# Cached keys summed head by head inside the heads of a hybrid decoder layer, a pooling tile as filler of the last head, and the stage behind in a new order

## The chip, the cores and the metric

One core of one Trainium2 chip runs the whole layer as one program. The metric is the time of one execution on the device in microseconds (us), the median of several. Engines are called by their names or by the profile's: TensorE (PE, with PEld for its weight loads), VectorE (DVE), ScalarE (ACT), GpSimd (POOL) and SyncE (SP), which here only issues DMAs.

## The reference

One decoder layer serves 1024 prompt tokens and 8 sample tokens (one new token for each of 8 sequences that have 512 cached tokens). Per layer:

```python
h = rms_norm(x, g_mix); z = h @ w_in        # [pool 512 | q 1024 | k 1024 | v 1024 | two gates 2048]
q, k = rope(z[q]), rope(z[k])               # 8 heads, two maps (c) of 64 per head
s = einsum('bqhcd,bkhcd->bhcqk', q, k) * 64 ** -0.5   # samples: k, v = cached pages + own token
p = softmax(masked s); a = p[:, :, 0] - lam * p[:, :, 1]
o = rms_norm(einsum('bhqk,bkhe->bqhe', a, v), g_subln) * (1 - lam_init)
pool_out = pool_mixer(z[pool])              # windows 2/4/8/16, mean minus token, map per group, scale
merged = sigmoid(gate1) * (pool_out @ w_pool_proj) + sigmoid(gate2) * (o @ w_attn_proj)
x = x + merged @ w_o
x = x + square(relu(rms_norm(x) @ w_up)) @ w_down; y = rms_norm(x)
```

Outputs are y for both groups, the new keys and values, and the last 15 rows of the pooling input. All is float32. The cached keys and values lie in pages of 128 tokens x 8 heads x 128 numbers, 4 pages per sample, found through a page table.

## The kernel before

Every engine has its own program; all order between them is by semaphores (names `s_...`), written out by hand. Each large product is made of three passes of a float32 split into a high and a low part: high x high, high x low, low x high. ScalarE makes the high part of the weights (`w_hi`, L1038), VectorE the low part (`w_lo`, L1347, `next_low`). Tokens are the 1032 columns, in three chunks of 344 (`passes`, L666).

**Heads.** After the first norm comes a loop over 8 heads of 9 steps (`head`, on each engine). Step s of head h does scores of query tile s (L602, L606), maxima (L1233) and exponentials (L946), the weights of the two maps (`weights`, L1243 to L1248), their transposes (L625) with `aT_hi` and `aT_lo` (L953, L1255), the value product of tile s-2 (L635), and beside it the projection of q, k, v of token tile s for head h+1 (L580), which VectorE rotates (`rotate`, L1218 to L1222) and GpSimd completes (`rotated`, L1646 to L1650) into `kv_st`. A staging buffer `kv_st` per parity holds nine tiles; `store_kv` (L399 to L405) stores them when all nine are ready. At a head's start ScalarE and VectorE split the next projection weights (`split_qkv`, L916, L1182). The last head (h = 7) has no projection beside it; at its last step three thirds of the first pooling product are put in (`first_product`).

**The stage behind.** `PART_A` lists 16 tiles: u is the product of a group of pooling channels (8 blocks of k, 72 matmuls), grp its 128x128 map (9 matmuls), gate a tile of the first gate (72) and pool a tile of `w_pool_proj` (36). Four gates and four pools stand in that list and four more pairs in a loop behind it. Two sets of three PSUM banks alternate; a tile's set is released through `s_free`. `pooling` (L1368 to L1384) makes windows, `pooled_low` (L1389) the low part `pl_lo`, for which grp waits; `y_hi` (L1078) and `y_lo` (L1458) are the map's output. Gate tiles go through the one buffer `gate`.

The cached keys are worked on in this stage. For each sample b, `load_keys` brings four pages of 128 tokens x all heads (2 MB) into one of two slots of `kv_pages` and the sample's q, spread over partitions, into `q_bc`. GpSimd multiplies three pages (L1684), VectorE the fourth (L1406) and sums all of them (`sum_keys`, L1410) at the tiles that `REDUCE_AT` names. Behind the last sum come the samples' softmax (`sample_softmax`), `select_weights`, and then the cached values through the same two slots: VectorE weighs two pages (L1491), GpSimd two (L1690), VectorE adds them (L1498, L1500), TensorE sums over partitions (`cached_values`, L799). The own scores of the samples (`own_scores`, L1395 to L1400) come after the second u tile.

Then come the attention gates and projections, w_o, the MLP and the last norm, which the change leaves alone.

Of the kernel before, what the change touches and what calls it, by code (L numbers as in the profile page):

```python
# [12 lines left out]
P = 128  # L13
D = 1024
# [55 lines left out]
def decoder_layer(nc, ins, outs):  # L70
# [48 lines left out]
    kv_st, _ = put("kv_st", [P, 2, NTT + 1, 2, P], F32)  # L119
# [25 lines left out]
    end_attn = cursor[0]  # L145

# [18 lines left out]
    up, a = put("up", [P, PAD + TOK], F32, r3)  # L165
# [10 lines left out]
    smp_q, _ = put("smp_q", [P, D], F32, tmp)  # L176
    smp_k, _ = put("smp_k", [P, D], F32, r4 - 4 * D)
# [7 lines left out]
    q_bc = [put("q_bc0", [P, D], F32, slot2[1])[0], put("q_bc1", [P, D], F32, slot2[2])[0]]  # L185
# [5 lines left out]
    wg_raw, a = put("wg_raw", [P, NG, P], F32, max(a, end_attn))  # L191
    inv_n, a = put("inv_n", [P, 16], F32, a)
    us, a = put("us", [P, NG, DEC, 16], F32, a)
    ufix, ufix_end = put("ufix", [P, 32], F32, a)
    tail_st, a = put("tail_st", [P, D_POOL], F32, slot2[0])
    state, a = put("state", [P, D_POOL], F32, a)
    a = ufix_end
    sc_all, a = put("sc_all", [P, PAGES, P], F32, a)
    sm_w, a = put("sm_w", [P, PAST], F32, a)
    a_all, a = put("a_all", [P, PAGES, DEC * HEADS], F32, a)  # L200
    sel, a = put("sel", [P, DEC * HEADS], F32, a)
    eye8, a = put("eye8", [P, DEC], F32, a)
    own, a = put("own", [P, DEC, 16], F32, a)
    own_s, a = put("own_s", [P, 16], F32, a)
# [29 lines left out]
    with ExitStack() as ctx:  # L234
# [26 lines left out]
        s_kv = [sem(f"kv_stored{i}") for i in range(2)]  # L261
# [8 lines left out]
        s_prod2, s_vs, s_vp = sem("k_products_dve"), sem("v_steps"), sem("v_products")  # L270
# [51 lines left out]
        PG_K = 16 * (PAGES + 1) * DEC // 2  # L322
# [8 lines left out]
        SET = (3, 0)  # L331
# [19 lines left out]
        def gate_tile(i):  # L351
            return later(S_LOOP // 2 + i, 0)

        def pool_tile(i):
            return later(S_LOOP // 2 + i, 1)
# [25 lines left out]
        def _(sp):  # L381
# [14 lines left out]
            def store_kv(h, par):  # L396

                sp.wait_ge(s_qk, 9 * h + 9)
                sp.wait_ge(s_zfree, 9 * h + 9)  # L399
                st = kv_st[:, par]  # L400
                sp.dma_start(kp_out[:, :, h], st[:, 0:NTT, 0]).then_inc(s_kv[par], 16)
                sp.dma_start(vp_out[:, :, h], st[:, 0:NTT, 1]).then_inc(s_kv[par], 16)
                sp.dma_start(new_k_s[0, :, 0, h], st[0:DEC, NTT, 0]).then_inc(s_kv[par], 16)
                sp.dma_start(new_v_s[0, :, 0, h], st[0:DEC, NTT, 1]).then_inc(s_kv[par], 16)
                sp.dma_start(q_scr[:, bass.ds(h * P, P)], qs_st[0:DEC, par]).then_inc(s_kv[par], 16)  # L405
# [33 lines left out]
            w_down0 = w_down[0].rearrange("(g k p) n -> p g k n", p=P, g=FG)  # L439
            sources = [(w_pool, NG, n) if kind == "pool" else (w_in0, KT, n + (OFF_G // P if kind == "gate" else 0))  # L440
                       for kind, n in PART_A if kind != "grp"]

# [6 lines left out]
            def load_pages(b, slot, cache):  # L449
                for g in range(PAGES):  # L450
                    page = sp.value_load(pages[0:1, bass.ds(b * PAGES + g, 1)], min_val=0,
                                         max_val=cache_k.shape[1] - 1)
                    sp.dma_start(kv_pg[:, slot, g],
                                 cache[0, bass.ds(page, 1)].rearrange("a s h e -> s (a h e)")).then_inc(s_pg[slot], 16)

            def load_keys(b):
                need(sp, s_kred, b - 1)
                load_pages(b, b % 2, cache_k)
                sp.dma_start(q_bc[b % 2][:], q_scr[b:b + 1].to_broadcast([P, D])).then_inc(s_pg[b % 2], 16)
# [3 lines left out]

            sp.wait_ge(s_const, N_CONST)
            store_kv(HEADS - 2, 0)
            sp.wait_ge(s_wlo, W_QKV)
            load_a(0)
            load_a(1)
            sp.dma_start(wg_raw[:], w_pool_grp[0].rearrange("g c d -> c g d")).then_inc(s_in2, 16)
            sp.dma_start(inv_n[:], c_inv).then_inc(s_in2, 16)  # L470
            sp.dma_start(state[0:DEC * BUF], state_pool[0].rearrange("b r c -> (b r) c")).then_inc(s_state, 16)
            store_kv(HEADS - 1, 1)
            load_a(2)
            load_a(3)
            sp.dma_start(new_pool_s[0, :, 0:BUF - 1], state_pool[0, :, 1:BUF]).then_inc(s_out, 16)
            sp.wait_ge(s_one, 2 * HEADS)
            for s_ in s_kv:
                sp.wait_ge(s_, 80 * HEADS // 2)
            sp.dma_start(smp_q[0:DEC], q_scr).then_inc(s_smp, 16)
# [11 lines left out]
            for l in range(4, 2 * lb):  # L491
                freed = [s_ for s_, kind, n, t in part_a() if 2 * t[2] + t[3] == l - 4 and kind != "grp"][0]
                while at < DEC - 2 and REDUCE_AT[at] < freed:
                    load_keys(at + 2)
                    at += 1
# [1258 lines left out]
```

## Time and profile before

| | us |
|---|---|
| median of 3 runs (lowest, highest) | 1842.93 (1841.47, 1843.98) |
| the profiled execution, its time | 1843.01 |
| its span, first to last instruction | 1841.2 |
| TensorE busy | 1772.3 |
| VectorE busy | 935.5 |
| ScalarE busy | 544.3 |
| GpSimd busy | 244.4 |
| mean granted clock of TensorE | 0.982 |

Stretches of the span: up to about 66 us the first norm and head 0's projection; up to 510 us heads 0 to 6; up to about 555 us the last head's scores; up to 808 us the stage behind; then attention gates, w_o, MLP and output. A granted clock of 1.00 is 2.4 GHz, 0.50 is 1.2 GHz. An instruction's idle time is how long its engine stood before it, and what follows the arrow is what ended that. Times in a view are us from the span's start.

### The profile page before, as it was taken

What the parts mean: (1) busy time and instruction counts of PE and PEld (TensorE: products, weight loads), DVE (VectorE), ACT (ScalarE), POOL (GpSimd) and SP (SyncE); (2) the same over time, 40 slices, a digit from 0 to 9 for tenths busy, and PEclk for the clock granted to TensorE, in tenths of its full rate; (3) what the DMA queues carried; (4) which work ended last, traced back from release to release, by engine and by line L of the source; (5) the groups of instructions that cost most, each with busy time, mean ns of one, the idle gap of its engine ahead of it and who ended that gap; (6) DMA issues with size and microseconds to landing.
All of it is one profiled execution on the core that took longest, in us unless ns stands there. A gap on an engine that the chain in (4) does not pass through costs nothing.

```text
span 1841.2 us, 27590 instructions
## 1 busy us (share of the span) xinstructions
PE 1772.3 (96%) x11428; PEld 1711.4 (93%) x11428; DVE 935.5 (51%) x1404; ACT 544.3 (30%) x1040; POOL 244.4 (13%) x284
## 2 busy tenths in 40 slices
PE   7999999999969699999999999999999999999997
PEld 6899888988959698999999999999999999999997
DVE  5677777777765987672225434421442244224323
ACT  4355545454543212121113332211220122012202
POOL 3211221222102554520000000000000000000001
PEclk9999999999989898999999999999999999999999
DMA  6211220222024474651122221111111111111112
GB/s 191 59 41 30 70 59 12 70 70 58 13 63 146 135 261 155 217 202 57 46 58 78 74 57 46 46 46 47 46 46 47 46 47 57 47 35 46 58 46 93
DMA packets 177988, 139.03 MB, mean 76 GB/s; under 512 B 7232, under 2 KB 163840, under 8 KB 177855
## 3 DMA queue, kind: packets, MB, share of 16 engines
q1 hardware_dynamic: 176711, 133.07, 23.8%
q10 hardware_dynamic: 1152, 4.19, 0.6%
q8 instruction: 91, 1.49, 0.3%
q14 instruction: 34, 0.28, 0.0%
HBM read 120.29 MB, written 17.18 MB: 75 GB/s over the span
## 4 chain that ended last, share of the span: by engine, by line
PE 82%; DVE 9%; issue 4%; ACT 2%; POOL 1%; DMA 1%; SPq 1%; DVEq 0%; ACTq 0%
PE ps L666 60%; PE ps L580 13%; PE ps L635 3%; PE ps L602 2%; PE ps L625 1%; DVE w_lo L1182 1%; DVE mx L1233 1%; POOL o_rstd L1662 1%; DMA w_raw<-in_w_in 1%; DVE win L1368 1%; DVE y_st L1624 1%; PE ps L799 1%; POOL kv_pages L1684 0%; DVE w_lo L1347 0%; DVE o_st L1268 0%
## 5 line engine op out<-in xcount | busy, mean ns | idle before, releaser
L666 PE MATMUL ps<-h_hi,w_hi 128*128 128x344 f32 x1248 | 270.2, 325 | 7.3 <-DVE w_lo L1347 3.8
L666 PE MATMUL ps<-h_lo,w_hi 128*128 128x344 f32 x1248 | 268.2, 324 | 0.0
L666 PE MATMUL ps<-h_hi,w_lo 128*128 128x344 f32 x1248 | 267.0, 323 | 0.0
L1038 ACT ACTIVATE w_hi<-w_raw 128x1024 fp32r<-128x1024 f32 x106 | 111.9, 1055 | 443.7 <-PE ps L666 439.1
L666 PEld LDWEIGHTS ps<-h_hi,w_hi 128*128 128x128 f32 x1248 | 213.5, 192 | 8.1 <-DVE w_lo L1347 4.1
L666 PEld LDWEIGHTS ps<-h_lo,w_hi 128*128 128x128 f32 x1248 | 214.0, 191 | 0.0
L666 PEld LDWEIGHTS ps<-h_hi,w_lo 128*128 128x128 f32 x1248 | 211.4, 191 | 0.0
L580 PE MATMUL ps<-w_hi,h_hi 128*128 128x384 f32 (+1 forms) x576 | 202.1, 351 | 4.2 <-DVE w_lo L1182 3.7
L580 PE MATMUL ps<-w_hi,h_lo 128*128 128x384 f32 (+1 forms) x576 | 195.7, 340 | 0.0
L580 PE MATMUL ps<-w_lo,h_hi 128*128 128x384 f32 (+1 forms) x576 | 194.9, 338 | 0.0
L1347 DVE TENSOR_TENSOR w_lo<-w_raw,w_hi 128x1024 fp32r<-128x1024 f32 x106 | 138.6, 1308 | 81.5 <-ACT w_hi L1038 81.5
L1604 DVE TENSOR_TENSOR x<-ps,x 128x1032 f32<-128x1032 f32 x32 | 39.5, 1233 | 269.7 <-PE ps L666 269.7
L666 PE MATMUL ps<-ff_lo,w_hi 128*128 128x344 f32 x768 | 162.9, 320 | 0.0
L666 PE MATMUL ps<-ff_hi,w_hi 128*128 128x344 f32 x768 | 162.9, 320 | 0.0
L666 PE MATMUL ps<-ff_hi,w_lo 128*128 128x344 f32 x768 | 162.2, 319 | 0.0
L1592 DVE TENSOR_TENSOR scaled<-relu,r_bc 128x1032 f32<-128x1032 f32 x32 | 39.5, 1234 | 183.9 <-ACT relu L1154 175.2
L666 PEld LDWEIGHTS ps<-ff_lo,w_hi 128*128 128x128 f32 x768 | 130.0, 189 | 0.0
L666 PEld LDWEIGHTS ps<-ff_hi,w_hi 128*128 128x128 f32 x768 | 129.3, 188 | 0.0
L666 PEld LDWEIGHTS ps<-ff_hi,w_lo 128*128 128x128 f32 x768 | 127.9, 188 | 0.0
L946 ACT ACTIVATE prob<-ps,nbias 128x256 f32<-128x256 f32 (+7 forms) x128 | 95.0, 742 | 83.7 <-DVE nbias L1236 81.2
L580 PEld LDWEIGHTS ps<-w_hi,h_hi 128*128 128x128 f32 (+1 forms) x576 | 102.7, 178 | 10.3 <-issue 4.2
L580 PEld LDWEIGHTS ps<-w_hi,h_lo 128*128 128x128 f32 (+1 forms) x576 | 102.4, 178 | 5.5
(221 smaller groups left out, 2782.6 us busy)
## 6 DMA issues: line engine op xcount, KB each, us to landing
w_raw<-in_w_in SPq DMA_DIRECT2D x44, 512.0 KB, 5.5
kv_pages<-in_cache_k SPq DMA_DIRECT2D x32, 512.0 KB, 5.1
kv_pages<-in_cache_v SPq DMA_DIRECT2D x32, 512.0 KB, 5.0
w_raw<-in_w_up SPq DMA_DIRECT2D x32, 512.0 KB, 4.0
w_raw<-in_w_down SPq DMA_DIRECT2D x32, 512.0 KB, 3.6
out<-kv_st SPq DMA_DIRECT2D x16, 512.0 KB
x_in<-in_x_prompt SPq DMA_DIRECT2D x8, 512.0 KB, 5.3
attention_out_scratch<-oT_st ACTq DMA_DIRECT2D x8, 512.0 KB, 2.7
```

Of the source, the lines that this page charges most:

```text
L580: mm = pe.matmul(bank[0:n, 0:3 * P], a[:, kt, toks(t)], w[:, :, kt, :], start=(kt == 0 and m == 0), stop=(kt == KT - 1 and m == 2))
L602: pe.matmul(bank_s[:, c, 512 * b:512 * b + n], q[part, par, 0, i * P:(i + 1) * P], k[part, par, 1, 512 * b:512 * b + n], start=(m == 0), s ...
L625: mm = pe.transpose(bank_t[r][:, (k - 4 * r) * P:(k - 4 * r + 1) * P], prob[:, i % 2, 0, k * P:(k + 1) * P], ident[:])
L635: mm = pe.matmul(bank_o[:, 0:2 * P], a[:, k * P:(k + 1) * P], v_hl[:, par, k].rearrange("p s e -> p (s e)"), start=(k == 0 and m == 0), st ...
L666: mm = pe.matmul(ps[:, SET[sp] + c, 0:CH], w, a[:, c * CH:(c + 1) * CH], start=(first and m == 0), stop=(last and m == 2))
L799: mm = pe.matmul(ps[:, 6, bass.ds((2 * i + slot) * HEADS + h, 1)], kv_pg[:, slot, 0, h * P:(h + 1) * P], ones[:, 0:1], start=True, stop=True)
L946: act.activation(prob[:, i % 2, c, 0:n], bank_s[:, c, 0:n], ACT.Exp, bias=nbias[:, i % 2, c:c + 1], scale=SCALE, accum_out=sums[:, i, c:c ...
L1038: act.activation(w_hi[:, lp], w_raw[:, lp], ACT.Copy).then_inc(s_whi, 1)
L1182: dve.tensor_tensor(w_lo[:, :, part], w_raw[:, :, part], w_hi[:, :, part].bitcast(F32), ALU.subtract).then_inc(s_wlo, 1)
L1347: dve.tensor_tensor(w_lo[:, lp], w_raw[:, lp], w_hi[:, lp].bitcast(F32), ALU.subtract).then_inc(s_wlo, 1)
L1592: dve.tensor_tensor(scaled[:], relu[:], r_bc[:], ALU.mult).then_inc(s_frr, 1)
L1604: dve.tensor_tensor(x1_chunks[:, n], psum_set(t[1]), x1_chunks[:, n], ALU.add).then_inc(s_free[t[1]], 1)
```

## The change

Five things change together.

1. The cached keys move into the heads. `load_keys(h, b)` brings the four pages of sample b, only the 128 columns of head h, into one of four slots of a new ring `key_ring`; `spread_q(h)` brings all samples' q of head h into `q_bc`. GpSimd multiplies one sample at a time (512 numbers per partition), VectorE sums it one step later.
2. To make room, `kv_st` becomes a ring of four tiles, each stored as soon as it is rotated (`store_tile`); `rotate` waits for the store of four tiles before.
3. The product of the first pooling tile is computed in the last head, in thirds of 344 columns through `bank_z`, in 24 units of three matmuls that `FILL` spreads over the steps. `first_product` at step 8 is now the second pooling tile. The two w_hi and w_lo of the last head's front move to its steps 0 and 3, and the samples' own scores to its steps 3 to 5.
4. `PART_A` is shorter (2 gates and pools instead of 4) and in another order; gate tiles run from 7 down to 0; gates but one are written straight into `merged` and multiplied there. The samples' softmax comes after the third pooling tile, and the cached values are spread over the later gate and pool tiles (`VALUES_AFTER`).
5. The key products and sums are gone from the stage. The sample's norms move into gate 0.

```diff
+PART_A = [("u", 0), ("u", 1), ("u", 2), ("grp", 0), ("u", 3), ("grp", 1), ("gate", 7), ("grp", 2), ("gate", 6), ("grp", 3),
+          ("pool", 7), ("pool", 6)]
+N_A = 2
+KV_RING = 4
+KEY_RING = 4
+KEYS_AT = {2: (0, 1), 3: (2, 3), 4: (4,), 5: (5,), 6: (6,), 7: (7,)}
+VALUES_AFTER = {("pool", 6): 0, ("gate", 5): 1, ("gate", 4): 2, ("pool", 4): 3, ("pool", 3): 4, ("gate", 2): 5,
+                ("pool", 2): 6, ("gate", 1): 7}
+FILL = {(1, 0): 2, (1, 1): 1, (2, 0): 2, (2, 1): 1, (3, 0): 2, (3, 1): 1, (4, 0): 2, (4, 1): 1, (5, 0): 2, (5, 1): 1,
+        (6, 0): 1, (6, 1): 1, (7, 0): 2, (7, 1): 2, (8, 0): 3}
...
 SyncE
+            def load_keys(h, b):
+                need(sp, s_kred, DEC * h + b - KEY_RING + 1)
+                slot = key_slot(h, b)
+                for g in range(PAGES):
+                    sp.dma_start(kc[:, slot, g], cache_k[0, bass.ds(page_of(b, g), 1), :, h].rearrange(
+                        "a s e -> s (a e)")).then_inc(s_kc[slot], 16)
+            for h in range(HEADS - 1):
+                spread_q(h)
+                for s in range(NTT + 1):
+                    store_tile(h + 1, s)
+                    if s == 1 and h < HEADS - 2:
+                        load_qkv(h + 2)
...
+                    keys_behind(h, s)
 TensorE
+            def fill(s, place):
+                for unit in range(filled[0], filled[0] + FILL.get((s, place), 0)):
+                    c, kt = unit // KT, unit % KT
+                    if unit == 0:
+                        pe.wait_ge(s_zfree, 9 * HEADS)
+                        pe.wait_ge(s_wlo, W_QKV + 1)
+                    elif kt == 0:
+                        pe.wait_ge(s_u0e, c)
+                    cols_ = slice(c * CH, (c + 1) * CH)
+                    for m, (w, a) in enumerate(((w_hi, h_hi), (w_hi, h_lo), (w_lo, h_hi))):
+                        mm = pe.matmul(bank_z[:, 0:CH], w[:, 0, kt], a[:, kt, cols_], start=(kt == 0 and m == 0),
+                                       stop=(kt == KT - 1 and m == 2))
...
+            state_transposes()
+            first_product(6, KT)
+            product(u_tile(2), h_hi, h_lo, KT, between={3: last_head_out, 6: own_transposes, 7: lambda: tail_transpose(0)})
+            group(0)
+            product(u_tile(3), h_hi, h_lo, KT, between={1: score_transposes, 3: lambda: tail_transpose(1)})
+            group(1)
+            gate_product(7, {1: select_weights, 3: lambda: tail_transpose(2)})
+            group(2)
+            gate_product(6, {3: lambda: tail_transpose(3)})
+            group(3)
+            pool_product(7)
+            pool_product(6)
+            for n in range(KT - N_A - 1, -1, -1):
+                gate_product(n, {2: sample_norms, 6: spread_norms} if n == 0 else None)
+                pool_product(n)
 VectorE
+            def sum_keys(h, b):
+                dve.wait_ge(s_prod, DEC * h + b + 1)
+                dve.tensor_reduce(sc_all[:, :, b * 16 + 2 * h:b * 16 + 2 * h + 2],
+                                  kc[:, key_slot(h, b)].rearrange("p g (c e) -> p g c e", c=2), AX_X,
+                                  ALU.add).then_inc(s_kred, 1)
 in head, at the end of step s
+                    for b in KEYS_AT.get(s - 1, ()):
+                        sum_keys(h, b)
+                    if not proj and s in (0, 3):
+                        low(s // 3)
+                    if not proj and 3 <= s <= 5:
+                        own_step(s - 3)
 in rotate
-                if t == 0:
-                    need(dve, s_kv[par], 80 * k_par)
+                need(dve, s_kv[kv_slot(hp, t)], 32 * kv_uses(hp, t))
 GpSimd
+            def key_products(h, b):
+                slot = key_slot(h, b)
+                pool.wait_ge(s_qb, 16 * (h + 1))
+                pool.wait_ge(s_kc[slot], 16 * PAGES * (key_uses(h, b) + 1))
+                pool.tensor_tensor(kc[:, slot], kc[:, slot], q_bc[:, b].unsqueeze(1).to_broadcast([P, PAGES, P]),
+                                   ALU.mult).then_inc(s_prod, 1)
```

## Rows read from the trace of the kernel before

**Rows 1.** The page: TensorE's busy time, and its granted clock in 40 slices.
```profile
PE 1772.3 (96%) x11428; PEld 1711.4 (93%) x11428; DVE 935.5 (51%) x1404; ACT 544.3 (30%) x1040; POOL 244.4 (13%) x284
PEclk9999999999989898999999999999999999999999
```

**Rows 2.** Busy time by stretch: a middle head and the last head.
```profile
core 0: us, PE busy (x) PEld busy (x) DVE busy (x) ACT busy (x) POOL busy (x), PEclk, DMA share, GB/s
320.00:383.00 63.00, 62.91 (x432) 56.40 (x431) 46.50 (x115) 31.95 (x90) 13.31 (x27) 1.00 0.18 52
510.00:560.00 50.00, 33.61 (x207) 27.66 (x207) 34.54 (x81) 24.54 (x68) 2.52 (x3) 0.80 0.19 58
```

**Rows 3.** Busy time by stretch: the stage behind, two of six stretches, and all six.
```profile
600.00:655.00 55.00, 38.92 (x218) 38.08 (x219) 51.27 (x40) 13.79 (x16) 26.23 (x10) 0.81 0.54 177
711.00:762.00 51.00, 48.09 (x303) 46.99 (x302) 41.31 (x27) 9.65 (x13) 24.39 (x8) 0.93 0.48 160
...
sum 253.40, PE 227.28 PEld 223.94 DVE 197.88 ACT 52.38 POOL 119.29; mean PE 37.88 PEld 37.32 DVE 32.98 ACT 8.73 POOL 19.88
```

**Rows 4.** The chain of waits, three pieces: start us, us, engine, line, instructions.
```profile
692.25 14.20 PE ps L666 x72
...
806.35 1.84 PE ps L799 x16
...
815.32 144.80 PE ps L666 x916
```

**Rows 5.** Instructions of TensorE in time order, those behind the longest waits.
```profile
609.45 1.23 PE L666 MATMUL ps<-pl_hi,wg_hi 128*128 128x344 f32 x3 [7.33 <-DVE pl_lo L1389]
644.40 1.23 PE L666 MATMUL ps<-pl_hi,wg_hi 128*128 128x344 f32 x3 [7.11 <-DVE pl_lo L1389]
692.25 1.23 PE L666 MATMUL ps<-h_hi,w_hi 128*128 128x344 f32 x3 [3.84 <-DVE w_lo L1347]
```

**Rows 6.** Groups by shape, 575 to 815 us, VectorE and ScalarE: busy, mean ns.
```profile
L1410 DVE TENSOR_REDUCE sc_all<-kv_pages 128x64 f32<-128x4096 f32 x8 | 35.4, 4420 | 2.6 <-POOL kv_pages L1684 2.4
L1406 DVE TENSOR_TENSOR kv_pages<-kv_pages,q_bc 128x1024 f32<-128x1024 f32 x8 | 20.7, 2588 | 0.0
L1458 DVE SCALAR_TENSOR_TENSOR y_lo<-ps,cols,y_hi 128x1032 fp32r<-128x1032 f32 x4 | 5.1, 1284 | 0.0
L1038 ACT ACTIVATE w_hi<-w_raw 128x1024 fp32r<-128x1024 f32 x20 | 21.1, 1053 | 35.0 <-PE ps L666 30.4 <-DMA w_raw<-in_w_pool_proj 4.6
L1078 ACT ACTIVATE y_hi<-ps,cols 128x1032 fp32r<-128x1032 f32 x4 | 4.5, 1120 | 16.3 <-PE ps L666 16.3
```

**Rows 7.** GpSimd's key products (ns min/median/max), and VectorE as they start.
```profile
L1684 POOL TENSOR_TENSOR kv_pages<-kv_pages,q_bc x24: 2342/2768/3537, 589.8 to 694.4; 128x1024 f32<-128x1024 f32 x24
L1406 DVE TENSOR_TENSOR kv_pages<-kv_pages,q_bc x8: 1206/3396/3430, 601.4 to 695.4; 128x1024 f32<-128x1024 f32 x8
...
590.20 2.16 DVE L1382 SCALAR_TENSOR_TENSOR pooled<-ufix,us 128x8 f32<-128x8 f32 x1
...
592.35 3.43 DVE L1347 TENSOR_TENSOR w_lo<-w_raw,w_hi 128x1024 fp32r<-128x1024 f32 x1
```

**Rows 8.** Instructions of VectorE in the last head.
```profile
511.45 2.54 DVE L1342 TENSOR_TENSOR w_lo<-w_raw,w_hi 128x1024 fp32r<-128x1024 f32 x2 [0.31 <-ACT w_hi L1031]
513.91 0.28 DVE L1233 TENSOR_REDUCE mx<-ps 128x1 f32<-128x128 f32 x1
...
525.83 0.69 DVE L1233 TENSOR_REDUCE mx<-ps 128x1 f32<-128x512 f32 x1
...
532.22 0.83 DVE L1233 TENSOR_REDUCE mx<-ps 128x1 f32<-128x640 f32 x1 [1.56 <-PE ps L606]
```

**Rows 9.** VectorE in a late step, and both engines at a head's start.
```profile
373.22 0.35 DVE L1261 SCALAR_TENSOR_TENSOR o_st<-ps,rsum,o_low 128x128 f32<-128x128 f32 x1 [1.53 <-ACT o_low L959]
...
383.74 3.83 DVE L1182 TENSOR_TENSOR w_lo<-w_raw,w_hi 128x768 fp32r<-128x768 f32 x4
...
384.93 0.19 PEld L580 LDWEIGHTS ps<-w_hi,h_hi 128*128 128x128 f32 x1
```

**Rows 10.** SyncE issues, in time order: four pages of a sample, a head's k.
```profile
579.61 3.74 SPq L453 DMA_DIRECT2D kv_pages<-in_cache_k  x4
...
385.05 0.39 SPq L401 DMA_DIRECT2D out<-kv_st  x1
```

**Rows 11.** All waits of TensorE from 66 to 510 us: in total, times, longest.
```profile
PE ps L580 <- DVE w_lo L1182: 2.0, 1, 2.0
```

More of the change, by code:

```diff
@@ L486, in _ @@
-            load_keys(1)
             n_gate = OFF_G // P
-            lb = (S_LOOP - NG) // 2
-            at = 0
[L491 to L495, printed above, removed]
-                load_a(l)
-            for b in range(at + 2, DEC):
-                load_keys(b)
-            sp.wait_ge(s_tailc, 1)
@@ L514, in _ @@
-            sp.wait_ge(s_out, 48)
-            sp.dma_start(x_smp[0:DEC], xs_).then_inc(s_xs, 16)
-            for i in range(DEC // 2 - 1, KT - N_A - 1):
-                load(lb + 1 + i, 0, w_in0, KT, n_gate + N_A + 1 + i)
-                load(lb + 1 + i, 1, w_pool, NG, N_A + 1 + i)
+            for l in range(6, len(sources)):
+                load_a(l)
+                after = VALUES_AFTER.get(source_kinds[l - 4])
+                if after is not None and after + 2 < DEC:
+                    load_pages(after + 2)
+                if source_kinds[l] == ("pool", 5):
+                    sp.wait_ge(s_tailc, 1)
+                    sp.dma_start(new_pool_p[0, 0], tail_st[0:BUF]).then_inc(s_out, 16)
+                    sp.dma_start(new_pool_s[0, :, BUF - 1], tail_st[BUF:BUF + DEC]).then_inc(s_out, 16)
+                if source_kinds[l] == ("pool", 3):
+                    sp.wait_ge(s_out, 48)
+                    sp.dma_start(x_smp[0:DEC], xs_).then_inc(s_xs, 16)
@@ L705, in head @@
                         weight_transposes(h, s - 1, 1, proj)
+                    if not proj:
+                        fill(s, 1)
                     if normed and s == 3:
@@ L823, in _, with group @@
-            pe.wait_ge(s_vout, 2)
-            for i in range(0, DEC // 2):
-                product(gate_tile(i), h_hi, h_lo, KT)
-                cached_values(i, 0)
-                product(pool_tile(i), y_hi, y_lo, NG)
-                cached_values(i, 1)
-            for i in range(DEC // 2, KT - N_A):
-                product(gate_tile(i), h_hi, h_lo, KT)
-                product(pool_tile(i), y_hi, y_lo, NG)
+            def group(g):
+                t = grp_tile(g)
+                pe.wait_ge(s_pllo, g + 1)
+                pe.wait_ge(s_wglo, 1)
+                need(pe, s_free[t[1]], t[0])
+                passes(t[1], wg_hi[:, g], wg_lo[:, g], pl_hi, pl_lo, True, True)
@@ new lines, in gate_product, with pool_product @@
+            def gate_product(n, between=None):
+                product(gate_tile(n), h_hi, h_lo, KT, between=between)
+                if ("gate", n) in VALUES_AFTER:
+                    cached_values(VALUES_AFTER["gate", n])
+            def pool_product(n):
+                if n == KT - 1:
+                    tile_out(pe, grp_tile(NG - 1))
+                product(pool_tile(n), y_hi, y_lo, NG)
+                if ("pool", n) in VALUES_AFTER:
+                    cached_values(VALUES_AFTER["pool", n])
@@ L986, in head @@
                         o_out(h - 1, 1 - par, NTT - 1)
+                    if not proj and s in (3, 6, 8):
+                        first_chunk_out(s // 3 - 1 if s < 8 else 2)
                     if s >= 1:
```

610 lines of the change are left out of this document (320 added, 290 removed).

## The prediction, made before the change was run

> **What bounds the kernel now.** I read the summary of the page first [rows 1]: TensorE is busy for 1772.3 of 1841.2 us, so only what idles it or slows it counts. Its granted clock falls in slices 12, 14 and 16 (between 506 and 737 us) and in no other. Busy time by stretch says the same [rows 2]: a middle head takes 63.0 us with TensorE busy for 62.9 and VectorE for 46.5; the last head, which has no projection beside it, takes 50 us with TensorE busy for 33.6 at a granted clock of 0.80.
>
> The stage behind, from the first pooling product at 554.8 us to the start of the first attention gate at 808.2 us, lasts 253.4 us. TensorE is busy for 227.3 of it [rows 3], so it idles for 26.1. Part of the busy time is spent at the 1.2 GHz level. How much: later 916 matmuls take 144.80 us, 0.158 us each [rows 4]. The stage has 4+8 products of 72 matmuls, 8 of 36 and 4 of 9, 1188 in all, so 187.8 us at that pace; eight sums of cached values at about 1.85 us [rows 4] are 14.8; the short rest (transposes, selection and the last head's two value products, summed from the chain's pieces) is 9.8. That is 212.4, and 227.3 - 212.4 = 14.9 us is the slow clock. The long waits are for VectorE: 7.33 and 7.11 us for pl_lo, 3.84 for w_lo [rows 5]; each is followed by matmuls at half pace (1.23 us for the three that take 0.64 elsewhere). VectorE is busy for 51.3 of 55 us between 600 and 655.
>
> What fills VectorE there: eight sums of keys at 4.42 us, eight products at 1.21 to 3.43 us, and two-input steps stretched from 1.2 to 3.4 us beside GpSimd's own key products of 2.34 to 3.54 us [rows 6, 7].
>
> **Part 1, the stage behind.** The keys leave it: 35.4 + 20.7 us of VectorE [rows 6] and 24 GpSimd products. The product of the first pooling tile leaves it too: 72 x 0.158 = 11.4 us. The floor is 212.4 - 11.4 = 201.0 us.
>
> Which waits remain? I laid out the new orders with the durations of [rows 6]. Group 0 needs pl_lo(0): u1 ends 20 us after the stage's start; copying up, w_hi, two copies of the head's output, wg_hi and pl_hi (about 10 us with their waits) come before it, while TensorE has 11.4 us of u2 and 2.5 us of transposes: no wait. Groups 1 and 2 have 5 to 8 us to spare, since only windows, one or two w_lo, the sample softmax and pl_lo stand on VectorE between them. The first wait that I find is the first pool product, which needs the last y_lo: ScalarE does the sigmoid (about 1.0), w_hi 1.05 and y_hi 1.12 us, then VectorE y_lo 1.28, together 4.5 us from the end of the gate product before, against 1.4 us of group 3 on TensorE: 3.1 us. After such a wait the clock is low: the 72 matmuls behind the 3.84 us wait took 14.20 us instead of 11.4 [rows 4, 5], so 2.8 more. For the last two cached samples, pages have to be loaded (about 8 us for four), weighed by GpSimd (twice 3.4) and summed (3.5) within some 20 us: 3 us for both. Together 9 us, bounds 3 and 25 (a wait of 7 with its slow clock, twice, as now). The stage becomes 210 us: **-43.4 us**.
>
> **Part 2, the last head.** It is a serial chain through VectorE: two maxima, ScalarE's exponentials, then aT_lo, ratio and prob, then the next maxima at once [rows 8]; TensorE waits in it. So what is put behind prob in a step delays the next maximum.
> - Gone from its front: two w_lo, 2.2 us (first maximum at 513.9, could start at 511.7). They come back in step 0 and step 3, each with its w_hi ahead on ScalarE (about 1.0): net +0.6 in step 0.
> - Step 3: two reduces, w_lo 1.3, the samples' own product 1.2, w_hi 1.0 and a third of the tile copied out (0.55), less 1.56 us for which VectorE waits for scores now [rows 8]: with the reduces below, 3.7.
> - Step 4: two reduces and own_s 1.2: 2.4. Step 5: 0.9. Step 6: a reduce and a copy, 1.15. The reduce in step 7 is behind the last exponentials.
>
> A reduce of 128x512 is not in the trace. An eighth of 4.42 is 0.55, and the maximum over 128x512 from PSUM takes 0.68 [rows 6, 8]; I take 0.60. The sum is 8.8; own's product can meet running GpSimd products, as a w_lo does now (3.43 against 1.2), 2.2 more: **+11 us**. Bounds 4 (the four pieces of scores of some 1.7 us on the chain at full clock, and own's product unblocked) and 18 (every reduce with a blocked step beside it). The 24 filling units of three matmuls (0.47 us each) lie in TensorE's idle time of 16.4 us; 11.4 fits if the clock stays up, and at half clock (22.8) some 6 would show, inside the upper bound.
>
> **Part 3, the seven heads before.** Each gets eight reduces, 4.8 us, and eight GpSimd products of 128x512; half of the 2.77 us of 128x1024 [rows 7] is 1.38, bounds 1.2 and 1.8. VectorE goes from 46.5 to 51.3 of 63 us. In late steps it waits 1.4 us and more before each o_st [rows 9], which takes the 0.6. At the end of a head it is different: the last reduce stands between qk_lo and the next split. The split's first quarter starts at 383.74 and is done at 384.70; TensorE takes it at 384.93 [rows 9]. 0.6 later is 0.4 late: 0.3 to 0.4 in each of seven heads, so **+2 us**. Bounds: nothing below 0, since TensorE is busy for 62.9 of 63 us and none of its work leaves; above, 12.
>
> What a product costs VectorE is read at its start: a step of 8 elements, normally 0.17 us, took 2.16 us, to the end of the first GpSimd product; the w_lo behind it 3.43, one more product and its own 1.2; the reduces stayed at 4.42 throughout [rows 6, 7]. So a blocked step waits for one product at most, 1.4 us here, and maxima and reduces don't wait. In the heads a product starts behind the rotation, beside qk_lo, reduce and maxima; only in steps 2 and 3, with two products each, does it reach ratio and prob, some 1 us per head, in VectorE's slack. The Trainium skill, "SBUF — State Buffer", section "SBUF: two separate sides", speaks against this change: a VectorE step with two SBUF inputs and a GpSimd step exclude each other, and the loser "fully blocks". By that rule, the trace agrees (2.16 against 0.17 us), the cost is a wait per meeting, 1 us per head. Were it bandwidth that is shared, all VectorE work beside the 11 us of products would stretch by 3.4/1.2, some 20 us per head, and VectorE would set the head.
>
> **Queues.** SyncE issues four pages in 3.7 us [rows 10], so 32 key loads cost 30 us per head; tile stores at 0.4 to 0.6 each, small stores at 1.2 to 1.3 and weights make 13: 43 of 63 us, against 6 now. A tile's store must have landed four tiles later, some 20 us; what waits behind the double loads (7.4 us in a 7 us step) is late by a step at most. DMA share in a head is 0.18 for 3.3 MB [rows 2]; 2.6 MB more makes about 0.32. Both hidden. The added waits: VectorE's rotation waits for the store of four tiles before (behind it the next maxima, and TensorE for those); its reduce waits for a product issued a step earlier; own_step waits for SyncE's load of smp_q, issued once the last stores landed, about 10 us before step 3 (behind it maximum 4); SyncE waits for s_kred, with the next tile's store behind it. I expect none to cost, with 5 us as the price of a late smp_q, inside the last head's bound. ScalarE loses two of three table loads (1.28 us each) off the path.
>
> **Sum.** 1843.0 (the profiled execution: span 1841.2 and 1.8 around it; median 1842.9) - 43.4 + 11 + 2 = 1812.6; I say **1812**. Its own range is 1800 to 1824.
>
> **Rivals.**
> - A, the last head hides more: with TensorE fed, its clock no longer drops to 1.2 GHz, its pieces on the chain shorten, and the stage behind comes near its floor. Last head +5, stage 204: 1843 - 49.4 + 5 + 0 = 1799. For it: clock 0.80 there; against it: the chain is VectorE's.
> - B, the wait moves to the cached values and late DMA: GpSimd's value products and two slots of pages stay, and after each wait the clock is low. As from 711 to 762 [rows 3], where 2.9 of 51 us are idle and the clock of 0.93 costs 3.6, a loss of 6.5 per 51 us makes 25 over the stage: 1843 - 27.4 + 13 = 1829.
> - C, the other sign: the seven heads become bound by VectorE. Eight reduces (0.60) and eight blocked steps (1.38) are 15.8 us per head, against 16.5 of VectorE idle, much of which is wait inside the chain that no added work can use. It decides from 32.4/7 = 4.6 us per head. At 7.5 us: 1812 + 50 = 1862. For it: the lock above, and the 3.8 us of split at a head's start [rows 9]; against it: no TensorE wait above 2.0 us in 444 us of heads [rows 11].
> - D, the filler doesn't fill: a third waits for bank_z to be copied by ScalarE behind the exponentials, and holds up TensorE in front of the scores, at half clock. Last head +22: 1824.
> - E, nothing moves, because what left returns elsewhere: 1843.
>
> **How the numbers follow.** Forecast 0.50, A 0.14, B 0.16, C 0.09, D 0.08, E 0.03. Low end: stage 205, last head +4, heads 0 gives 1799, and A a little better, 1793. High end: waits of 25, last head +14, heads +7 give 1837. C lies outside. No change is within 0.2% (3.7 us). Faster: forecast, A, B, D = 0.88; same 0.03; slower 0.09.
>
> **What would show it.** Right: a reduce on VectorE of about 0.60 us 64 times, each in a head; key products near 1.4 us; heads of 63 to 63.5 us; the last head some 60 us long with TensorE over 45 busy; no wait for pl_lo above 1 us; one wait of about 3 us ahead of the first pool product; the stage at 210 us. Wrong: heads of 65 us and more, TensorE waits for w_lo at their start or rc waiting for a store; a last head over 68 us; clock below 0.95 in the stage.

## The result and the profile after

The change takes 1847.4 us (median; 1842.9 before): ratio 1.0018, 95% interval 1.0010 to 1.0027. It is slower by a little, where 1812 was forecast. The profiled execution took 1847.7 us, with a span of 1845.8, 4.6 more than before.

The page of after, TensorE's busy time and its granted clock in 40 slices, against [rows 1]:

```profile
PE 1774.7 (96%) x11428; PEld 1709.0 (93%) x11428; DVE 911.6 (49%) x1452; ACT 539.0 (29%) x1040; POOL 246.4 (13%) x325
PEclk9999999999988999899999999999999999999999
```

TensorE is as busy as before (1772.3 us). To see where the time is, the kernel is cut at the instructions that begin a part. Instructions of VectorE after: the first quarter of the split that opens a head, for head 0, heads 1 and 2, and the last of the seven.

```profile
67.31 0.99 DVE L1282 TENSOR_TENSOR w_lo<-w_raw,w_hi 128x768 fp32r<-128x768 f32 x1
138.06 0.94 DVE L1282 TENSOR_TENSOR w_lo<-w_raw,w_hi 128x768 fp32r<-128x768 f32 x1
203.63 0.94 DVE L1282 TENSOR_TENSOR w_lo<-w_raw,w_hi 128x768 fp32r<-128x768 f32 x1
...
466.04 0.94 DVE L1282 TENSOR_TENSOR w_lo<-w_raw,w_hi 128x768 fp32r<-128x768 f32 x1
```

Head 0 takes 70.75 us and the next ones 65.6 each. Before, the same cuts gave 62.16 and 63.73 (one of them is the row at 383.74 in [rows 9]). Busy time by stretch, after: a middle head, the last head, a piece of the stage behind, and the whole of it, against [rows 2, 3].

```profile
core 0: us, PE busy (x) PEld busy (x) DVE busy (x) ACT busy (x) POOL busy (x), PEclk, DMA share, GB/s
334.86:400.48 65.62, 64.45 (x438) 57.00 (x437) 51.33 (x127) 32.43 (x91) 22.89 (x36) 1.00 0.38 90
531.60:585.80 54.20, 40.28 (x241) 34.70 (x241) 39.42 (x84) 24.92 (x69) 11.78 (x10) 0.81 0.30 76
...
745.00:790.00 45.00, 40.02 (x232) 39.52 (x231) 25.91 (x14) 5.01 (x5) 11.61 (x4) 0.86 0.38 129
...
585.80:813.90 228.10, 210.45 (x1336) 207.94 (x1336) 134.84 (x123) 46.13 (x59) 46.47 (x19) 0.95 0.38 129
```

| part | before | after | difference | predicted |
|---|---|---|---|---|
| ahead of the heads | 66.6 | 67.3 | +0.7 | 0 |
| head 0 | 62.2 | 70.8 | +8.6 | +0.3 |
| heads 1 to 5 | 318.7 | 328.0 | +9.3 | +1.4 |
| head 6 and the last head, to the first product that is alone | 107.3 | 119.8 | +12.5 | +11.3 |
| stage behind | 253.4 | 228.1 | -25.3 | -43.4 |
| rest | 1033.0 | 1031.8 | -1.2 | 0 |
| span | 1841.2 | 1845.8 | +4.6 | -30.4 |

The cut between the last head and the stage behind, 585.80 us, lies 0.2 us behind the start of that product in the trace (585.63); the two rows are as exact as that.
The last head opens without a split, so head 6 and it stand in one row; with head 6 like the five before (+1.85 each), the seven heads cost 19.7 us and the last head 10.6. Two parts are off: the seven heads by 17.7 us, the stage behind by 18.1.

**Head 0.** SyncE's issues, GpSimd's first key product and VectorE's first sum, three views of after:

```profile
69.58 17.39 SPq L453 DMA_DIRECT2D key_ring<-in_cache_k  x16
87.02 0.43 SPq L459 DMA_DIRECT2D q_bc<-q_sample_scratch  x1
```

```profile
95.54 2.52 POOL L1784 TENSOR_TENSOR key_ring<-key_ring,q_bc 128x512 f32<-128x512 f32 x2 [9.29 <-DMA q_bc<-q_sample_scratch]
```

```profile
96.87 0.69 DVE L1372 TENSOR_REDUCE sc_all<-key_ring 128x8 f32<-128x512 f32 x1 [5.26 <-POOL key_ring L1784]
```

The queries' spread stands behind 16 key loads in SyncE's order. GpSimd waits for it, VectorE's sum waits for GpSimd, and the next maxima stand behind the sums.

**Heads 1 to 6.** VectorE in a late step of a middle head, in time order:

```profile
301.85 0.41 DVE L1325 TENSOR_TENSOR qk_lo<-ps,qk_hi 128x256 fp32r<-128x256 f32 x1
302.18 1.27 DVE L1372 TENSOR_REDUCE sc_all<-key_ring 128x8 f32<-128x512 f32 x2
303.36 0.94 DVE L1332 TENSOR_REDUCE mx<-ps 128x1 f32<-128x768 f32 x1
...
306.87 0.35 DVE L1360 SCALAR_TENSOR_TENSOR o_st<-ps,rsum,o_low 128x128 f32<-128x128 f32 x1 [1.32 <-ACT o_low L1044]
```

The maxima start the moment the sums end, and the wait ahead of o_st is still there. ScalarE in the same step shows why: it waits for the maxima (nbias), and o_low stands behind both exponentials in its order, so late maxima make a late o_low.

```profile
304.53 0.90 ACT L1031 ACTIVATE prob<-ps,nbias 128x768 f32<-128x768 f32 x1 [2.26 <-DVE nbias L1335]
...
306.47 0.36 ACT L1044 ACTIVATE o_low<-ps,rsum 128x128 f32<-128x128 f32 x1
```

All of VectorE's waits for o_low in one middle head, in total, times and longest, before and after:

```profile
DVE o_st L1261 <- ACT o_low L959: 10.5, 8, 2.1
```

```profile
DVE o_st L1360 <- ACT o_low L1044: 9.6, 8, 1.5
```

Eight sums went into the head, and that idle time shrank by 0.9 us only. VectorE is busy for 4.2 us more (51.33 against 47.15 from 320.01 to 383.74), and the head is 1.9 longer. TensorE, which waited for nothing in the middle head before, now waits for VectorE's aT_lo:

```profile
PE ps L643 <- DVE aT_lo L1354: 1.1, 3, 0.4
```

That is the idle time of the head (64.45 us busy of 65.62, before 63.64 of 63.73). The waits are in the late steps; the wait for w_lo at a head's start, which the prediction named as the place of the cost, is there once in the seven heads, 2.0 us long, as before [rows 11].

**The stage behind.** TensorE's waits there, after:

```profile
PE ps L879 <- DVE kv_pages L1571: 8.4, 3, 4.5
PE ps L722 <- DVE y_lo L1548: 5.2, 1, 5.2
PE ps L722 <- DVE w_lo L1458: 2.1, 1, 2.1
PE ps L722 <- ACT up L1156: 2.0, 1, 2.0
```

No wait for pl_lo is left. The waits come to 17.7 us, and TensorE is busy for 210.5 against the floor of 201, so the slow clock costs 9.5. Losses of 27.1 us stand where 9 were expected; before they were 26.1 + 14.9 = 41.0 [rows 3]. SyncE's issues there, one of the six pairs of a tile and a sample's pages, and VectorE at the w_lo before that pair and ahead of two samples:

```profile
750.08 0.39 SPq L513 DMA_DIRECT2D w_raw<-in_w_pool_proj  x1
751.25 3.68 SPq L519 DMA_DIRECT2D kv_pages<-in_cache_v  x4
```

```profile
728.34 4.02 DVE L1562 TENSOR_TENSOR kv_pages<-kv_pages,a_all 128x2048 f32<-128x2048 f32 x1 [8.74 <-DMA kv_pages<-in_cache_v]
...
748.84 1.22 DVE L1458 TENSOR_TENSOR w_lo<-w_raw,w_hi 128x1024 fp32r<-128x1024 f32 x1
760.18 4.02 DVE L1562 TENSOR_TENSOR kv_pages<-kv_pages,a_all 128x2048 f32<-128x2048 f32 x1 [10.12 <-DMA kv_pages<-in_cache_v]
```

A sample's pages are issued only behind the load of a tile, which waits until the tile's slot is free of its w_lo: the w_lo at 748.84 ends at 750.06, and the tile's load is issued at 750.08.

### The profile page after: what moved, and what is told of

The parts are those of the page before. It is cut to its first block, busy times and chain, and to the rows that moved or that the text cites. A ratio compares the mean times of both kernels' runs of the same rounds, so it can differ in the third digit from the quotient of the medians.

```text
span 1845.8 us, 29274 instructions
## 1 busy us (share of the span) xinstructions
PE 1774.7 (96%) x11428; PEld 1709.0 (93%) x11428; DVE 911.6 (49%) x1452; ACT 539.0 (29%) x1040; POOL 246.4 (13%) x325
## 4 chain that ended last, share of the span: by engine, by line
PE 68%; DVE 17%; issue 6%; ACT 3%; DMA 2%; POOL 2%; SPq 1%; ACTq 0%; DVEq 0%; POOLq 0%
PE ps L722 59%; PE ps L636 6%; DVE mx L1332 4%; DVE aT_lo L1354 2%; DVE sc_all L1372 1%; DMA kv_pages<-in_cache_v 1%; DVE rc L1317 1%; DVE w_lo L1282 1%; POOL kv_pages L1813 1%; PE ps L691 1%; DVE rs L1319 1%; ACT aT_hi L1038 1%; DVE qk_lo L1325 1%; ACT prob L1031 1%; POOL o_rstd L1789 1%
## 5 line engine op out<-in xcount | busy, mean ns | idle before, releaser
L722 PE MATMUL ps<-h_hi,w_hi 128*128 128x344 f32 x1224 | 263.5, 324 | 4.1 <-DVE w_lo L1458 2.1
L722 PE MATMUL ps<-h_lo,w_hi 128*128 128x344 f32 x1224 | 261.0, 322 | 0.0
L722 PE MATMUL ps<-h_hi,w_lo 128*128 128x344 f32 x1224 | 259.8, 321 | 0.0
L722 PEld LDWEIGHTS ps<-h_hi,w_hi 128*128 128x128 f32 x1224 | 206.8, 190 | 4.8 <-issue 2.3
L722 PEld LDWEIGHTS ps<-h_lo,w_hi 128*128 128x128 f32 x1224 | 208.4, 190 | 0.0
L722 PEld LDWEIGHTS ps<-h_hi,w_lo 128*128 128x128 f32 x1224 | 205.2, 189 | 0.0
L1458 DVE TENSOR_TENSOR w_lo<-w_raw,w_hi 128x1024 fp32r<-128x1024 f32 x106 | 134.1, 1265 | 88.8 <-ACT w_hi L1127 88.8
L636 PEld LDWEIGHTS ps<-w_hi,h_hi 128*128 128x128 f32 (+1 forms) x576 | 102.8, 178 | 11.7 <-issue 5.5
```

Source lines behind the costliest of these rows:

```text
L636: mm = pe.matmul(bank[0:n, 0:3 * P], a[:, kt, toks(t)], w[:, :, kt, :], start=(kt == 0 and m == 0), stop=(kt == KT - 1 and m == 2))
L722: mm = pe.matmul(ps[:, SET[sp] + c, 0:CH], w, a[:, c * CH:(c + 1) * CH], start=(first and m == 0), stop=(last and m == 2))
L1458: dve.tensor_tensor(w_lo[:, lp], w_raw[:, lp], w_hi[:, lp].bitcast(F32), ALU.subtract).then_inc(s_wlo, 1)
```

## The experiments

Ratios are against the kernel before, run beside each (the changed kernel four times, ten times in e2 and e3). The lengths of heads and stages are of the profiled execution, one of each kernel. T is the time from the first product that is alone to ScalarE's sigmoid of the second attention gate: 289.2 us before, 262.3 after (the stage behind and the first attention tile).

### The sum's length (e1)

```
-   kc[:, key_slot(h, b)].rearrange("p g (c e) -> p g c e", c=2), AX_X,
+   kc[:, key_slot(h, b)].rearrange("p g (c e) -> p g c e", c=2)[:, :, :, 0:2], AX_X,
```

> The changed kernel, with each of the 64 sums of a sample's keys in the heads taken over 16 numbers per partition and not 512 (the sample's scores are wrong by that). Theory chain (VectorE's in-order loop maxima, exponentials, aT, prob sets the late steps of a head, so the 0.68 us behind prob delays the next maxima): heads 1 to 6 fall from 65.6 to 63.7 us each, the last head by 2 to 3 us, in all 11 to 14 us less than the changed kernel; the stall of 5 to 9 us in head 0 stays. Theory lock (GpSimd's products hold VectorE's two-input steps): the products are all still there, so heads stay at 65.5 and the time within 2 us.

Measured: 1830.0 us, ratio 0.9937 (0.9913 to 0.9962). The sums by line (ns min/median/max, first and last start), and the openings of heads 1 and 2:

```profile
L1372 DVE TENSOR_REDUCE sc_all<-key_ring x64: 147/160/171, 95.9 to 574.1; 128x8 f32<-128x16 f32 x64
```

```profile
134.06 0.96 DVE L1282 TENSOR_TENSOR w_lo<-w_raw,w_hi 128x768 fp32r<-128x768 f32 x1
197.82 0.96 DVE L1282 TENSOR_TENSOR w_lo<-w_raw,w_hi 128x768 fp32r<-128x768 f32 x1
```

A middle head is back at 63.8 us, with every product of GpSimd still there. The length of the sums was what the heads paid for. Eight times 0.52 us less gives 1.8 back, and no more could come back: 63.8 us is what TensorE's own work takes (63.64 us busy of 63.73 before). How much of each sum is on the loop is therefore not shown, only that the lengthening is theirs. Head 0 keeps 68.1, and the last head became 5 us shorter, more than the 2 to 3 expected; in all the time is 17.4 us below after, where 11 to 14 were expected.

### The product's length (e2)

```
-   pool.tensor_tensor(kc[:, slot], kc[:, slot], q_bc[:, b].unsqueeze(1).to_broadcast([P, PAGES, P]),
+   pool.tensor_tensor(kc[:, slot, 0, 0:8], kc[:, slot, 0, 0:8], q_bc[:, b, 0:8],
```

> The changed kernel, with each of the 64 GpSimd products in the heads taken over 8 numbers per partition and not 512 (scores of the samples wrong by that); waits, loads and sums stay. Theory lock: heads 1 to 6 fall to 63.7 us. Theory chain: they stay at 65.4 to 65.6 us, and only the last head, where VectorE waits for a product, gives 1 to 3 us.

Measured: 1840.2 us, ratio 0.9989 (0.9979 to 1.0000). GpSimd's products by line (in after, 64 of 128x512 with a median of 1288 ns):

```profile
L1784 POOL TENSOR_TENSOR key_ring<-key_ring,q_bc x64: 193/203/707, 93.8 to 569.5; 128x8 f32<-128x8 f32 x64
```

The middle heads stay at 65.6 us: the products cost them nothing. Head 0 is 1.7 us shorter without them (70.75 to 69.09) and the last head 3.9 (54.2 to 50.3). The last head shows where: three steps of VectorE start while a product runs. One of them, and GpSimd's products under it, in after, and then the same step in e2:

```profile
548.99 2.50 POOL L1784 TENSOR_TENSOR key_ring<-key_ring,q_bc 128x512 f32<-128x512 f32 x2
...
550.53 0.97 DVE L1344 SCALAR_TENSOR_TENSOR ratio<-sums,nlam,rsum 128x1 f32<-128x1 f32 x1
```

```profile
547.16 0.22 DVE L1344 SCALAR_TENSOR_TENSOR ratio<-sums,nlam,rsum 128x1 f32<-128x1 f32 x1
```

The step ends with the product (both at 551.5). The other two are a prob at 560.34 (1.93 us against 0.88 in e2) and a ratio at 569.47 (0.73 against 0.22); together the three take 2.3 us more. The rest of the 3.9 is no more than the length of the last head changes with the granted clock between two runs (3.2 us, see e8).

### The queries' spread ahead of the key loads (e3)

```
             sp.wait_ge(s_const, N_CONST)
+            spread_q(0)
             for b in range(KEY_RING):
```

> The changed kernel, with SyncE issuing head 0's spread of q ahead of the sixteen first key loads and not behind them. Theory queue (head 0 takes 70.75 us and not 62.2 because the first product waits for q, issued at 87 us behind 17.4 us of key issues, and VectorE's first sum stands in front of maxima for 5.3 us): head 0 falls to 63 to 65 us, the time by 6 to 8 us, all else as it was. Rival: head 0 pays for the late stores and weights that stand behind the same issues, and stays above 68 us.

Measured: 1840.8 us, ratio 0.9991 (0.9977 to 1.0005), 6.6 below after. SyncE's issues, and the openings of heads 0 and 1:

```profile
67.60 0.39 SPq L459 DMA_DIRECT2D q_bc<-q_sample_scratch  x1
69.04 17.22 SPq L453 DMA_DIRECT2D key_ring<-in_cache_k  x16
```

```profile
66.12 3.61 DVE L1284 TENSOR_TENSOR w_lo<-w_raw,w_hi 128x768 fp32r<-128x768 f32 x4
...
130.88 3.54 DVE L1284 TENSOR_TENSOR w_lo<-w_raw,w_hi 128x768 fp32r<-128x768 f32 x4
```

Head 0 falls from 70.8 to 64.8 us. One issue in the wrong place had cost 6.0 of its 8.6 us; the other 2.6 go with the sums (e8 has head 0 at 62.15).

### The sums moved into the wait for o_low (e4)

The sums run one step later, ahead of o_st instead of ahead of the maxima; SyncE's refills move with them.

```
                         normed_head(h - 1, 1 - par)
+                    for b in KEYS_AT.get(s - 2, ()):
+                        sum_keys(h, b)
                     if s >= 2:
...
                         qk_low(h + 1, 1 - par, s - 1)
-                    for b in KEYS_AT.get(s - 1, ()):
-                        sum_keys(h, b)
```

> The changed kernel, with the sums of keys one step later and moved from behind prob and the rotation to where VectorE waits 1.0 to 1.5 us for ScalarE's o_low (in the last step, ahead of the rotation). All work stays. Theory chain: heads 1 to 6 fall from 65.6 to 63.7 to 64.2 us, the last head by 3 us, head 0 by 0 to 5; 11 to 16 us less in all. Theory that VectorE simply has too much to do: 65.6 stays, as the same 5.4 us per head are there.

Measured: 1827.9 us, ratio 0.9921 (0.9897 to 0.9945), with all the work of after. VectorE in a late step:

```profile
297.41 1.27 DVE L1372 TENSOR_REDUCE sc_all<-key_ring 128x8 f32<-128x512 f32 x2
298.82 0.35 DVE L1360 SCALAR_TENSOR_TENSOR o_st<-ps,rsum,o_low 128x128 f32<-128x128 f32 x1
```

VectorE's waits for o_low in a middle head:

```profile
DVE o_st L1360 <- ACT o_low L1044: 5.9, 6, 1.2
```

Now the idle time takes the sums (10.5 us before, 9.6 after, 5.9 here), and a middle head is at 63.8 us. Same instructions, other place: 1.8 us per head. The time is 19.5 us below after, more than the 11 to 16 expected: head 0 is 3.1 shorter, heads 1 to 6 together 10.9 and the last head 3.9.

### The kernel before, with its key arithmetic cut (e5)

```
-    part = kv_pg[:, b % 2, g]
-    pool.tensor_tensor(part, part, q_bc[b % 2][:], ALU.mult).then_inc(s_prod, 1)
+    part = kv_pg[:, b % 2, g, 0:8]
+    pool.tensor_tensor(part, part, q_bc[b % 2][:, 0:8], ALU.mult).then_inc(s_prod, 1)
```

and VectorE's product and sum cut in the same way.

> The kernel before, with its key products (8 numbers per partition in place of 1024) and key sums (2 of 64 numbers of each row) cut down in the stage behind; page loads, waits and order stay (the samples' scores are wrong by that). It prices the key arithmetic alone. If VectorE's and GpSimd's key work made the stage's idle and slow 41 us, the stage of 253.4 us falls to 215 to 225 and the time to 1805 to 1815. If the order and the page loads made it, the stage stays above 238 and the time above 1828.

Measured: 1813.4 us, ratio 0.9851 (0.9834 to 0.9869). Busy time over the stage behind, and what is left of TensorE's wait for pl_lo in it:

```profile
554.00:778.00 224.00, 218.52 (x1402) 216.07 (x1403) 136.95 (x140) 52.18 (x67) 57.87 (x42) 0.97 0.60 206
```

```profile
PE ps L666 <- DVE pl_lo L1389: 0.2, 1, 0.2
```

The key arithmetic was worth 29.6 us to the stage behind (T 259.6), and the 7 us waits for pl_lo were its work. With the tile that the change takes out of the stage (11.4 us), 41 us could leave it, near the predicted 43.4. T fell by 26.9, so some 14 of them were lost to the change's own order. That is a difference of sums of three runs; e7 and e8 find the places.

### All filler at the last head's end (e6)

```
-FILL = {(1, 0): 2, (1, 1): 1, (2, 0): 2, (2, 1): 1, ... (7, 0): 2, (7, 1): 2, (8, 0): 3}
+FILL = {(8, 0): 24}
```

The copies out of the tile go to step 8 with it.

> The changed kernel, with all 24 filling units in step 8 of the last head, and the three copies of the tile there. It prices the filler. If the idle time of TensorE in steps 1 to 7 hid the product's 11.4 us for nothing, this kernel is 8 us slower than the changed one (some 3 us of step 8 are idle anyway). If the filler held up the last head's chain (its waits for up and w_lo are 8.1 us), the last head up to step 8 shortens and the difference is 0 to 4 us.

Measured: 1855.5 us, ratio 1.0078 (1.0061 to 1.0095), 8.1 above after by the medians, 5.6 by the profiled executions. The last head, and TensorE's largest wait in it:

```profile
531.10:593.40 62.30, 40.61 (x239) 34.16 (x238) 42.47 (x88) 24.91 (x69) 11.73 (x10) 0.81 0.25 66
```

```profile
PE ps L658 <- ACT prob L1031: 14.8, 6, 3.7
```

That wait was 5.8 us in after. The last head is 8.1 us longer (62.3 against 54.2). So the filler does fill: spread out, it hides some 8 us of the tile's 11.4. The granted clock is 0.81 whether it is spread or not.

### Sums in the wait, spread first, pages first (e7)

e3 and e4 together, and a sample's pages issued ahead of the tile's load:

```
             for l in range(6, len(sources)):
-                load_a(l)
                 after = VALUES_AFTER.get(source_kinds[l - 4])
...
                     load_pages(after + 2)
+                load_a(l)
```

> The changed kernel with the sums of keys in VectorE's gap, q ahead of the first key loads, and in the stage behind each pair of cached value pages issued ahead of the weights load that it followed. Heads: head 0 62 to 63.5 us, the others 63.75, 1821 us from these two. Theory pages (the waits of 8.4 us for cached values and their slow clock come from pages issued 3 to 8 us late behind a wait for w_lo): 8 to 12 us more, 1810 to 1813. Rival (GpSimd's products of 5.8 us and two slots bound it): within 3 us of 1821.

Measured: 1808.0 us, ratio 0.9818 (0.9799 to 0.9836). TensorE's waits in the stage behind, and VectorE's for the pages:

```profile
PE ps L724 <- DVE y_lo L1553: 5.2, 1, 5.2
...
PE ps L881 <- DVE kv_pages L1576: 1.5, 1, 1.5
```

```profile
DVE kv_pages L1567 <- DMA kv_pages<-in_cache_v: 6.7, 3, 4.6
```

The 8.4 us for the sampled values are 1.5, VectorE's 26.6 us for pages are 6.7, and T is 249.3 against 262.1 in e4. The place of six groups of issues was worth 12.8 us. Head 0 is at 63.7, the middle heads at 63.8.

### y_lo ahead of the first sample's values (e8)

```
             next_low(gate_tile(7))
-            weigh_values(0)
-            sum_values(0)
             next_low(gate_tile(6))
             group_low(3)
+            weigh_values(0)
+            sum_values(0)
```

> As the kernel before this, with VectorE making the last y_lo ahead of the first cached value's weighing and sum, and not behind their 5.8 us. Theory: the wait of 5.2 us ahead of the first pool product falls to 2 to 3 us, and the slow clock behind it goes or shrinks: 3 to 6 us less than that kernel. Rival: the first cached values come later and TensorE waits for them instead, no difference.

Measured: 1808.0 us, ratio 0.9813 (0.9797 to 0.9829): no difference from e7.

```profile
PE ps L724 <- DVE y_lo L1553: 3.1, 1, 3.1
```

The wait is the 3.1 us that the prediction worked out, so the other 2.1 in after were VectorE weighing and adding values in front of y_lo. T is 2.5 shorter, but the 3 to 6 us expected of the time did not come: the last head, which the edit does not touch, is 3.2 longer in this profiled execution, and head 0 1.5 shorter. Both differences go with TensorE's granted clock, the only difference that the traces show in these two stretches. The end of the last head, from the same point of it (39.81 us behind its start), in e7 and in e8:

```profile
552.00:560.49 8.49, 7.91 (x57) 7.22 (x58) 6.58 (x12) 4.76 (x13) 2.59 (x2) 1.00 0.46 127
```

```profile
551.35:563.05 11.70, 10.68 (x58) 9.26 (x58) 8.16 (x17) 5.84 (x17) 2.54 (x2) 0.71 0.53 145
```

The same work takes 8.5 us at 1.00 and 11.7 at 0.71. At the start of head 0 e7 has a short stretch at the lower level (0.89 from 60.00 to 76.00, against 1.00 from 60.90 to 76.90 in e8). In e8 the heads cost nothing any more: heads 0 to 5 take 380.9 us, as before.

### Filler shifted within the last head (e9), and values earlier (e10)

e9, on e8:

```
+FILL = {(1, 1): 2, (2, 0): 3, (2, 1): 1, (3, 0): 2, (4, 0): 3, (4, 1): 1, (5, 0): 3, (5, 1): 1,
+        (7, 0): 3, (7, 1): 2, (8, 0): 3}
```

> As e8_plus_y_low_first, with the filling units laid so that none comes in step 1 ahead of the transposes, and none of a new third in the step in which ScalarE copies the third before (3 and 6 stay partly or wholly empty); 24 units as before. TensorE's waits for up (5.4 us) and for w_lo (2.5 us) in the last head should go. Theory: these waits hold up scores and transposes, and the last head (some 50 us from its start to the first full product, 43.6 in the kernel before) falls by 2 to 5 us. Rival: they lie beside VectorE's own loop, which sets the last head, and the time stays within 1 us.

Measured: 1805.9 us, ratio 0.9798 (0.9771 to 0.9824), the lowest time of all. TensorE's waits from 500 to 815 us:

```profile
PE ps L660 <- ACT prob L1033: 4.5, 2, 2.9
...
PE ps L702 <- DVE aT_lo L1356: 3.0, 1, 3.0
...
PE ps L683 <- DVE prob L1349: 1.3, 1, 1.3
```

The waits for ScalarE's copies of the tile (5.4 us in e8) are gone, and 4.3 us for aT_lo and prob have come. The last head is 2.8 us shorter than e8's and 0.4 longer than e7's, so it cannot be put down to the new places. The 2 us of the time lie inside the intervals of e8 and e9.

In e10, on e9, TensorE sums the first two samples' values one tile earlier, so that SyncE can issue the pages of the next two one tile earlier; VectorE's order stays:

```
-VALUES_AFTER = {("pool", 6): 0, ("gate", 5): 1, ("gate", 4): 2,
+VALUES_AFTER = {("pool", 7): 0, ("pool", 6): 1, ("gate", 4): 2,
```

> As e9, with TensorE summing the first two cached values one tile earlier (behind the first and the second pool product), so that their page slots come free some 7 us sooner. If pages still set the stage behind (one wait of 1.7 us for a cached value is left in it), 1 to 3 us less than e9; if the stage is at its floor apart from the first pool product's wait, no difference within 1 us.

Measured: 1807.3 us, ratio 0.9805 (0.9778 to 0.9831): no difference.

## Why the prediction was wrong

**The seven heads, +2 predicted, +19.7 measured: the step that failed first.** The claim was that VectorE "waits 1.4 us and more before each o_st [rows 9], which takes the 0.6". A wait takes work only if the work stands in it. The sum stood behind qk_lo, ahead of the maxima. Maxima, exponentials, o_low, o_st, aT_lo, prob and the maxima again follow one another across VectorE and ScalarE, and the wait for o_low is time in that loop. Work put elsewhere in the loop pushes everything behind it, the wait included. Measured: the waits went from 10.5 to 9.6 us with the sums ahead of the maxima and to 5.9 with the sums inside them (e4), and 1.8 us per head went with the move. e1 gives the same from the other side. The size of a sum was mis-sized little (0.676 us, 0.60 taken), and VectorE's busy time came to the 51.3 us of the prediction: what was wrong is how much of the rest was free. That "TensorE is busy for 62.9 of 63 us and none of its work leaves" was used to bound the cost from below, and rightly; it says nothing of the other side: TensorE's work sets a head only while the loop of the others is shorter.

**The added waits, "I expect none to cost".** The list named rotation, sums, own_step and s_kred, and left out the queries' spread of head 0: the first key product needs a load which stands behind 16 issues. The rate was on hand (four in 3.7 us [rows 10], so 15 for 16; 17.4 measured). e3 gives 6.0 us back.

**GpSimd's products.** Sized 1.38 us, measured 1.288. That they cost the middle heads nothing held: 65.6 us with products and without (e2). That a product costs VectorE one wait per meeting held in the last head: three meetings, 2.3 us together. The Trainium skill, "SBUF — State Buffer", section "SBUF: two separate sides", says that a VectorE step with two SBUF inputs and a GpSimd step that reads SBUF exclude each other for the whole instruction; the trace agrees, a ratio of 0.22 us took 0.97 and ended with the product.

**The last head, +11 predicted, +10.6 measured.** The method, to count what VectorE does behind prob, gave the size, and the filler lies in idle time (e6). Part of the agreement is luck. The 2.2 us for the samples' own product beside a running GpSimd product did not come (it took 1.21 us, at 554.54), and 2.3 us came for ratio and prob instead, which were not in the sum. The filler leaves 8.1 us of waits for its own copies and w_lo (5.5 and 2.6), which were not in it either. And the same last head took 48.3 us in e7 and 51.5 in e8, with the same work and another granted clock.

**The stage behind, -43.4 predicted, -25.3 measured: the second step that failed.** The waits for pl_lo ended as forecast, and e5 shows that the key arithmetic had made them. What was mis-sized is "3 us for both" of the last cached samples. The prediction priced loading, weighing and summing, and not when a load can be issued: it follows a tile's load that waits for a w_lo. Placing the issues in front gives back 12.8 us (e7). In the wait for y_lo the chain of 3.1 us was worked out right, and what stands in front of it on VectorE was left out: weighing and adding the first sample's values, 5.8 us (2.28, 2.29 and 1.22), behind which y_lo starts 2.2 us after its y_hi is ready (e8). After both, T is 246.8, against 289.2 - 43.4 = 245.8, and the stage takes 212.7 us (563.00 to 775.70) with TensorE busy for 205.6 at a mean clock of 0.98. That is an estimated 201.5 us at full clock, against the floor of 201.

**The rivals.** The number is E's (1843), but not its reason. The mechanisms are two together: B's, late pages with a slow clock (its term -27.4, measured -25.3), and C's sentence that the idle time is "wait inside the chain that no added work can use", at 2.8 us per head on average and not the 7.5 it was priced at; 4.6 was not reached, and B's loss brought the sum over the line. Half of C's sentence is too strong: e4 shows work that does use it. A fell: the last head's clock is 0.81 where it was 0.80. D fell: it had the last head at +22, and e6 shows the filler filling.

**Left open.** What puts the stretches of the lower clock where they fall in one execution and not in another, and so whether e9 is better than e8; and how much of a sum lies on the loop, since TensorE's own work hides the rest.

## What to carry to other kernels

Idle time in front of an instruction is room only for work that stands in that very place of the engine's order; ahead of the instruction that starts the loop the same work lengthens every turn. So when work is added to an engine whose order is fixed, ask first which instruction it delays, then how busy the engine is. And of every load ask what stands in front of its issue: here two orders of issues cost 6.0 and 12.8 us, with VectorE busy for 49% of the span.

## What the hardware showed that was not expected

A sum of 128x512 took VectorE 0.676 us, where an eighth of the 4.42 us for 128x4096 would be 0.55. Sixteen loads of one head's keys (64 KB each) took SyncE 17.4 us to issue, 1.09 each, where groups of four loads of whole value pages (512 KB each) took 0.91 to 1.04 each (3.6 to 4.1 us), so the bytes of a load did not set its issue time here. And feeding TensorE more in the last head (40.3 us busy of 54.2, 33.6 of 50 before) did not raise its mean granted clock above 0.81. The clock of a part with waits is not a fixed price: the same last head had a mean of 0.89 in e7 and 0.83 in e8, and 3.2 us between them.
